# ScalarE rounds x times the norm's weights, and the squares are added by two additions

## What is computed

```python
def rmsnorm(x, g):
    xf = x.astype(jnp.float32)
    y = xf * lax.rsqrt(jnp.mean(xf * xf, axis=-1, keepdims=True) + EPS)
    return (y * g.astype(jnp.float32)).astype(x.dtype)

for i in range(DEPTH):                                    # first block
    x = x + 0.5 * swiglu_ffn(rmsnorm(x, ffn1_norm[i]), ffn1_wi[i], ffn1_wo[i])
    z = rmsnorm(x, mix_norm[i]) @ w_in[i]
    ...
    x = x + mixed @ w_out[i]
    x = x + 0.5 * swiglu_ffn(rmsnorm(x, ffn2_norm[i]), ffn2_wi[i], ffn2_wo[i])
    gate = jax.nn.sigmoid(rmsnorm(x, ple_norm[i]) @ w_ple_gate[i])
    x = x + gate * (p[i] @ w_ple[i])
for l in range(DEPTH):                                    # second block
    h = rmsnorm_2(x, norm_mix_g[l])
    ...
    x = x + mix @ w_out[l]
    x = x + squared_relu_mlp(rmsnorm_2(x, norm_mlp_g[l]), mlp_w1[l], mlp_w2[l])
return rmsnorm_2(x, final_norm_g)
```

## Time and profile before

| | us |
|---|---|
| median of 3 runs | 3871.23 |
| lowest and highest run | 3866.43, 3871.86 |
| span of the profiled execution | 3867.6 |
| its time beside the span | not given; the span is 3.6 under the median |
| PE busy | 3661.1 (95%) |
| POOL busy | 1404.7 (36%) |
| DVE busy | 1841.0 (48%) |
| ACT busy | 1006.2 (26%) |

### The profile page before, as it was taken

One profiled execution on the slowest core, in us unless ns is written; L12 is line 12 of the kernel. 1 busy time (PEld: TensorE's weight loads), 2 busy tenths in 40 slices (PEclk: granted clock), 3 DMA queues, 4 the chain that ended last, 5 costly groups with the idle time before them and its releaser, 6 DMA issues.

```text
span 3867.6 us, 44550 instructions
## 1 busy us (share of the span) xinstructions
PE 3661.1 (95%) x15582; PEld 2828.9 (73%) x15582; DVE 1841.0 (48%) x2258; ACT 1006.2 (26%) x1320; POOL 1404.7 (36%) x581
## 2 busy tenths in 40 slices
PE   3999999999999999999999999898899999889997
PEld 2888865778887788875678888664688876467886
DVE  3542224754424542323665422757463554748163
ACT  1222223322222222222422222333221123322111
POOL 1444432334443444331234443321244432114442
PEclk6999999999999999999999999888999998899998
DMA  3332321223322332231223323211133231113231
GB/s 92 106 98 93 96 68 49 71 82 98 98 97 86 96 96 94 84 90 44 66 78 101 98 98 96 71 32 30 54 104 97 94 87 37 36 44 91 94 98 60
DMA packets 473852, 309.79 MB, mean 80 GB/s; under 512 B 16809, under 2 KB 432531, under 8 KB 473715
## 3 DMA queue, kind: packets, MB, share of 16 engines
q1 hardware_dynamic: 470224, 305.16, 26.4%
q10 hardware_dynamic: 3491, 2.80, 0.5%
HBM read 304.25 MB, written 3.67 MB: 80 GB/s over the span
## 4 chain that ended last, share of the span: by engine, by line
issue 65%; POOL 24%; PE 9%; POOLq 1%; DVE 0%; ACT 0%; DVEq 0%
POOL wl L421 24%; PE bank L444 2%; PE bank L443 2%; PE bank L439 2%; PE bank L462 1%; PE bank L458 1%; PE bank L464 1%; POOLq L420 0%; POOLq L418 0%; PE bank L465 0%; DVE y_sb L2014 0%; PE mb L503 0%; DVE var L1444 0%; DVE var L1424 0%; POOLq L421 0%
## 5 line engine op out<-in xcount | busy, mean ns | idle before, releaser
L421 POOL TENSOR_TENSOR wl<-raw,wh 128x1024 fp32r<-128x1024 f32 x576 | 1404.3, 2440 | 2413.1 <-ACT wh L1093 2412.8
L1093 ACT ACTIVATE wh<-raw 128x1024 fp32r<-128x1024 f32 x576 | 607.1, 1056 | 1626.0 <-PE bank L458 793.6
L458 PE MATMUL bank<-xh,wh 128*128 128x512 f32 x2528 | 995.9, 394 | 3.5 <-DVE xl L1418 3.5
L462 PE MATMUL bank<-xl,wh 128*128 128x512 f32 x2528 | 990.2, 392 | 0.0
L464 PE MATMUL bank<-xh,wl 128*128 128x512 f32 x2212 | 866.5, 392 | 0.0
L458 PEld LDWEIGHTS bank<-xh,wh 128*128 128x128 f32 x2528 | 478.4, 189 | 119.3 <-issue 18.5
L462 PEld LDWEIGHTS bank<-xl,wh 128*128 128x128 f32 x2528 | 478.7, 189 | 99.2
L444 PE MATMUL bank<-hh,wl 128*128 128x512 f32 (+1 forms) x1216 | 485.1, 399 | 0.0
L464 PEld LDWEIGHTS bank<-xh,wl 128*128 128x128 f32 x2212 | 418.8, 189 | 88.8
L443 PE MATMUL bank<-hl,wh 128*128 128x512 f32 (+1 forms) x1216 | 479.2, 394 | 0.0
L439 PE MATMUL bank<-hh,wh 128*128 128x512 f32 (+1 forms) x1216 | 476.8, 392 | 0.0
(11 more groups left out here) (358 smaller groups left out, 3439.5 us busy)
## 6 DMA issues: line engine op xcount, KB each, us to landing
raw<-in_ffn_wi_dram SPq DMA_DIRECT2D x176, 512.0 KB, 3.8
raw<-in_mlp_w_dram SPq DMA_DIRECT2D x128, 512.0 KB, 3.8
raw<-in_w_in_dram SPq DMA_DIRECT2D x102, 512.0 KB, 3.7
raw<-in_ffn_wo_dram SPq DMA_DIRECT2D x88, 512.0 KB, 3.6
raw<-in_w_out_dram SPq DMA_DIRECT2D x32, 512.0 KB, 3.9
raw<-in_w_ple_gate_dram SPq DMA_DIRECT2D x16, 512.0 KB, 3.6
raw<-in_w_a_dram SPq DMA_DIRECT2D x8, 512.0 KB, 3.5
raw<-in_w_b_dram SPq DMA_DIRECT2D x8, 512.0 KB, 3.4
```

Source lines behind the costliest of these rows:

```text
L421: gp.tensor_tensor(wl[j][:], raw[j % RAW_SLOTS][:], wh[j][:].bitcast(F32), ALU.subtract)\
L458: first = pe.matmul(out[0:width, :], h[:, c:c + width], rh[:, k, :], start=k == 0, stop=False)
L462: pe.matmul(out[0:width, :], h[:, c:c + width], rl[:, k, :], start=False, stop=False)
L1093: act.activation(wh[n % SPLIT_SLOTS][:], raw[n % RAW_SLOTS][:], ACT.Copy).then_inc(s.hi_ready, 1)
```

## The change

On ACT, `square_half` is given the norm's weights. Before the Square it makes the `xh` of the half's first two x tiles and after it those of the last two, each by a Copy with a scale for each partition, and signals `xh_ready`. On DVE the `xh` product and its drain are gone, and each `xl` product waits for `xh_ready`. The strided reduction is replaced by an addition of two tiles to two tiles, a drain and an addition of one tile to one. In `first_half` DVE makes two `xl`, then the sum, then the other two, where it made all four ahead of the sum; in `norm` the order (two, sum, two) stays. The calls of `square_half`, `norm` and `ffn` on ACT pass the weights. Nothing else moves, so on ACT four copies stand between `x_final` and what followed the Square: in `norm`, the rounding of slab n+3.

```diff
+            def x_times_gain(j, g):
+                act.activation(xh[:, j, :], x_sb[:, j, :], ACT.Copy, scale=g[:, j:j + 1]).then_inc(s.xh_ready, 1)
 
-            def square_half(B, L, k, half):
+            def square_half(B, L, k, half, g):
                 act.wait_ge(s.x_final, half_no(B, L, k, half))
+                if g is not None:
+                    for j in range(4 * half, 4 * half + 2):
+                        x_times_gain(j, g)
                 if half:
                     act.wait_ge(s.ss_ready, half_no(B, L, k, 0))
                 act.activation(tmp_all[:], x_sb[:, 4 * half:4 * half + 4, :], ACT.Square).then_inc(s.sq_ready, 1)
+                if g is not None:
+                    for j in range(4 * half + 2, 4 * half + 4):
+                        x_times_gain(j, g)
...
-            def x_times_gain(j, g):
-                dve.tensor_scalar(xh[:, j, :], x_sb[:, j, :], g[:, j:j + 1], None, ALU.mult)
-                dve.drain()
+            def x_times_gain(B, L, k, j, g):
+                dve.wait_ge(s.xh_ready, at(L, B.norms * KT, B.base_norm * KT + k * KT + j + 1))
                 dve.scalar_tensor_tensor(out=xl[:, j, :], in0=x_sb[:, j, :], scalar=g[:, j:j + 1],
                                          in1=xh[:, j, :].bitcast(F32), op0=ALU.mult, op1=ALU.subtract)\
                    .then_inc(s.xl_ready, 1)
...
                 dve.wait_ge(s.sq_ready, half_no(B, L, k, half))
-                last = dve.tensor_reduce((acc, var)[half][:], tmp_all[:].rearrange("p j t -> p t j"), AX.X, ALU.add)
+                dve.tensor_tensor(tmp_all[:, 0:2, :], tmp_all[:, 0:2, :], tmp_all[:, 2:4, :], ALU.add)
+                dve.drain()
+                last = dve.tensor_tensor((acc, var)[half][:], tmp[0], tmp[1], ALU.add)
                 if half:
...
                 dve.drain().then_inc(s.x_final, 1)
                 if g is not None:
-                    for j in range(4):
-                        x_times_gain(j, g)
+                    for j in range(2):
+                        x_times_gain(B, L, k, j, g)
                 sum_half(B, L, k, 0)
+                if g is not None:
+                    for j in range(2, 4):
+                        x_times_gain(B, L, k, j, g)
```

More of the change, by code:

```diff
@@ L254, in program @@
             setup_t setup_copied rel_psum toep_row toep_out toep_in consts_ready
-            x_final sq_ready ss_ready ss_psum inv_var rstd_ready xl_ready
+            x_final sq_ready ss_ready ss_psum xh_ready inv_var rstd_ready xl_ready
             silu_done hidden_ready gate_landed gate_split gates_psum gate_pre log1p ml_rows_done emt_done
@@ L1106, in square_half, with norm @@
                 act.activation(tmp_all[:], x_sb[:, 4 * half:4 * half + 4, :], ACT.Square).then_inc(s.sq_ready, 1)
-            def norm(B, L, k, n):
-                square_half(B, L, k, 1)
+                if g is not None:
+                    for j in range(4 * half + 2, 4 * half + 4):
+                        x_times_gain(j, g)
+            def norm(B, L, k, n, g):
+                square_half(B, L, k, 1, g)
                 if n is not None:
@@ L1116, in norm, with ffn @@
                     ahead(B, L, n + 1, 3)
-            def ffn(L, k, n, t, silu0):
-                norm(Block1, L, k, n)
+            def ffn(L, k, n, t, silu0, g, g_next):
+                norm(Block1, L, k, n, g)
                 def pair(f, i=None):
@@ L1134, in ffn @@
                     ahead(Block1, L, n0, 4, i, 4)
-                square_half(Block1, L, k + 1, 0)
+                square_half(Block1, L, k + 1, 0, g_next)
                 with act.Fori(3, 5) as i:
@@ L1221, in gated @@
                 ahead(Block1, L, S_OUT, 5)
-                square_half(Block1, L, 2, 0)
+                square_half(Block1, L, 2, 0, par1[:, R_FFN2:R_FFN2 + KT])
                 ahead(Block1, L, S_OUT + 5, 3)
             def ple(L):
-                norm(Block1, L, 3, S_PLE)
+                norm(Block1, L, 3, S_PLE, par1[:, R_PLE:R_PLE + KT])
                 for j in range(KT):
@@ L1232, in ple @@
                         round_hi(Block1, L, S_PLE + j + AHEAD)
-                square_half(Block1, L, Block1.norms, 0)
+                square_half(Block1, L, Block1.norms, 0, g_first)
             for dst, name in ((rel, "rel_bias"), (onehot, "onehot"), (pad, "pad")):
@@ L1273, in _ @@
                .then_inc(s.toep_in, 16)
-            square_half(Block1, None, 0, 0)
+            square_half(Block1, None, 0, 0, g_first)
             with act.Fori(0, 2) as L:
@@ L1277, in _ @@
                     round_hi(Block1, L, n)
-                ffn(L, 0, S_FFN1, T_FFN1, 0)
-                norm(Block1, L, 1, S_IN)
+                ffn(L, 0, S_FFN1, T_FFN1, 0, g_first, par1[:, R_MIX:R_MIX + KT])
+                norm(Block1, L, 1, S_IN, par1[:, R_MIX:R_MIX + KT])
                 ahead(Block1, L, S_IN + 4, 8)
@@ L1283, in _ @@
                 gated(L)
-                ffn(L, 2, S_FFN2, T_FFN2, FT)
+                ffn(L, 2, S_FFN2, T_FFN2, FT, par1[:, R_FFN2:R_FFN2 + KT], par1[:, R_PLE:R_PLE + KT])
                 ple(L)
@@ L1395, in _ @@
                     round_hi(B, L, n)
-                norm(B, L, 0, S2_IN)
+                norm(B, L, 0, S2_IN, g_first)
                 gmlp(L)
@@ L1400, in _ @@
                 ahead(B, L, S2_OUT, 8)
-                square_half(B, L, 1, 0)
-                norm(B, L, 1, S2_MLP)
+                square_half(B, L, 1, 0, par2[:, Q_MLP:Q_MLP + KT])
+                norm(B, L, 1, S2_MLP, par2[:, Q_MLP:Q_MLP + KT])
                 with act.Fori(1, 2 * FT2 // 4 - 2) as i:
@@ L1405, in _ @@
                 ahead(B, L, B2_SLABS - 8, 2)
-                square_half(B, L, B.norms, 0)
+                square_half(B, L, B.norms, 0, g_first)
                 ahead(B, L, B2_SLABS - 6, 6)
-            norm(Last, None, 0, None)
+            norm(Last, None, 0, None, None)
         @block.vector
```

## The result

The median after is 3887.91 us (four runs, 3885.15 to 3890.14), beside 3869.70 for the kernel before in the same comparison: ratio 1.0049, 95% interval 1.0035 to 1.0063. It is slower, as forecast, and 2.9 us above the 3885 predicted. The forecast stood on a median of 3871.23, so the change itself came to +18.2 us where +14.1 was predicted. The span went from 3867.6 to 3886.5.

What follows compares the result with a forecast made beforehand. PE, busy 95%, loses time where it stands still, chiefly the fourth tile waiting for a slab rounded behind ACT's work. Terms 4.2 + 4.1 + 2.6 + 3.0 + 4.2 - 2.4 - 1.6 = +14.1 us on 3871.23 gave 3885, range 3880 to 3889.

Steps and rivals of the forecast that it cites:

- Startup: Ahead of the first loop: ACT rounds slabs later, so PE's fourth tile starts at 86.65 instead of 82.59, +4.1 us.
- Into Block2: Entry in layer 0: POOL's `wl` pair leaves the reduction's cover and stops DVE's x additions twice, +3.0 us.
- Block2 layer 1, k=0: That norm's fourth tile +2.5 us; PE's gap of 0.58 becomes 3.0, likely a cold restart, +1.7; together +4.2.
- Last norm: Program's last norm: no copies matter, PE waits for the sum, whose reduction becomes two additions, -1.6 us.
- k=1: Block2's norm k=1, in both layers: x final sooner, and PE's restart before the fourth tile warm, -1.2 us each.
- every fourth tile with a PE wait on POOL `wl`: Sign of being right: each fourth tile of `first_units` waits for its weight slab, 0.7 us at six Block1 norms.
- Six Block1 norms: Block1 norms k=1, 2, 3, two layers: copies delay the slab 2.5 us less 1.75 slack, +0.7 each, +4.2.
- 0 where the table below puts no POOL under the additions: Port-contention cost of DVE's additions per half, bounded 0 to 2.4 us, taken as 0 where no POOL runs beside them.
- PLE into layer 1: Entry into layer 1: x final 1.6 us sooner, then copies, fourth tile +0.9; PE's cold restart +1.7; together +2.6.
- Faster: Rival: DVE is what the norms wait for, so its cheaper sum wins; 3858 us, chance 0.12.
- The port lock: Rival: every sum in the open meets a `wl` and DVE gains nothing; about +21 us, 3892, chance 0.08.
- A wash: Rival: copies cost their low end (2.1), two gaps restart warm, collisions into Block2 luckier; +5 us, 3877, chance 0.25.

Runs made afterwards that it cites:

- additions only: The kernel before with only the two additions in place of the strided reduction, no copies on ACT: 3871.71 us, ratio 1.0014.
- copies only: The kernel after with the strided reduction back in both halves; ACT still makes the copies: 3893.42 us, ratio 1.0066.
- copies on the best version: The kernel before with additions in half 1 only, slab n+3 rounded ahead of the Square, and ACT's four copies per half: 3883.11 us, ratio 1.0035.

## Why the prediction was right

**Right, by its steps.** The slab's rounding behind ACT's Square is what the fourth tile waits for (the two kernels that move it take 14.6 and 15.9 us off the table's sum). Startup +4.3 for +4.1, first matmul at 73.97 for 74.0. The fourth tile at startup came at 86.70 for 86.65. Into Block2 +3.3 for +3.0, PE's start there 0.95 later for 1.15; Block2 layer 1, k=0, +4.1 for +4.2, with the cold restart: the matmuls after the wait of 3.14 take 0.63 each. Last norm -1.6 for -1.6. The copies cost 2.45 for 2.5.

**k=1: right in layer 0, by luck in layer 1.** -1.1 and -1.0 were measured for -1.2 (of which the terms given, +0.2 and -1.7, make -1.5). In layer 0 the fourth tile came 0.5 later, behind a wait of 1.82 on `wl`, and PE then ran warm (at its full clock), which won 1.6. In layer 1 PE came out of the second wait on `xl` cold (8 matmuls at 1.2 GHz), and the fourth tile waited for nothing. So of the sign "every fourth tile with a PE wait on POOL `wl`" this one is missing.

**Two terms were mis-sized, and by luck offset each other.** *Six Block1 norms*: 0.7 each predicted, 1.21 measured. The step that failed is "0 where the table below puts no POOL under the additions": it asked only whether `wl` would hold up DVE. At these norms it is DVE's third addition that holds up `wl`, by 0.37. The run with copies alone, where the reduction is back, shows 0.82.

*PLE into layer 1*: +2.6 predicted, +0.3 measured. Its parts failed too. The traces stand 8.08 us apart just before. Against that PE started 0.6 later (1261.34 - 1252.68 - 8.08), not 1.0 sooner. DVE was 2.2 sooner behind half 0, about as predicted, but the two additions ahead of the read that frees PE took 2.52 and 2.06, where they took 1.14 and 0.69: 2.75 more, where the prediction left room for 1.0. The last addition was held too (2.69). Yet x was final 2.5 sooner (predicted 1.6), since something else fell away. After its last addition, at the return of the loop over layers, DVE stood still with no releaser. Timeline of DVE, before:

```profile
1260.09 0.18 DVE L1730 COPY par<-p 128x38 f32 x1 [3.17 <-issue]
```

and after:

```profile
1255.34 2.52 DVE L1736 TENSOR_TENSOR x_sb<-x_sb,gate_sg 128x512 f32<-128x512 f32 x1
...
1258.56 2.06 DVE L1736 TENSOR_TENSOR x_sb<-x_sb,gate_sg 128x512 f32<-128x512 f32 x1
...
1262.69 2.69 DVE L1736 TENSOR_TENSOR x_sb<-x_sb,gate_sg 128x512 f32<-128x512 f32 x1
...
1265.77 0.18 DVE L1744 COPY par<-p 128x38 f32 x1 [0.39 <-issue]
```

The last addition ends 0.4 later, the return takes 2.8 less (0.39 for 3.17), so DVE is 2.4 sooner; then the copies (2.45) and a `wl` of 2.74 instead of 2.35 take it back: +0.3. What DVE does in that time is not shown, but the traces say when it shows. In the four kernels whose last addition took 0.69 (before, additions only, copies only, and copies on the best version) the idle time is 2.37 to 3.55; in the other eight traces `wl` held the last addition for 2.09 to 2.69, and the idle time is 0.39 to 1.25. So the return seems to run beside an addition that is held. With PE's wait at 2.00 instead of the 4.3 predicted, the cold restart (1.7) did not come.

Six norms cost 3.1 more, PLE 2.3 less, the rest agrees within 0.4 each; so the sum came out as 15.6 for 14.1. The prediction had no term for the stages between the norms, where the trace has another 3.5, the largest part with PE's clock. With them the change (+18.2 in the medians, +19.1 in the traces) lies above the +10 to +17 that the ends of the copies' price gave. The time lies within the forecast's 3880 to 3889 also because the kernel before came out 1.5 lower.

**The rivals.** *Faster* falls: with DVE's work taken away and the slab free, the copies still cost 17.7 us in the table (-6.0 to +11.7). *The port lock* got 0.08 and deserved more. Alone, the additions bring -0.7 instead of the -7 I expected of them: the lock eats them at both entries, as that rival said, but not at k=1 or at the last norm. *A wash* needed a ratio of 1.0015; the interval begins at 1.0035.

## What to carry to other kernels

Before work is moved to an idle engine, look at what is queued behind the place where it goes: ACT was idle 74% of the time, and yet its next instruction was the one that TensorE waited for. Before a slow instruction is replaced by faster ones, look at what lies beside it and which ports it leaves alone; a strided reduction of 3.7 us was the cover under which POOL worked undisturbed. Where instructions of two engines collide, ask in both directions who holds up whom, and where the stall goes once it is moved.

## What the runs showed of the hardware

- A shared port works in both directions, and the price depends on who is first. POOL first: DVE's addition of 1.22 took 3.36. DVE first: `wl` took 2.78 instead of 2.41. A reduction beside POOL cost neither more than 0.1: in the kernel before it took 3.62 to 3.82 without POOL and 3.70 to 3.91 beside it, and a `wl` that started under it 2.34 to 2.41.
- Not only two-input instructions are held up. A cast of DVE, one input, in the kernel before, beside a pair of `wl` (POOL's line) and alone:

```profile
3500.25 5.45 POOL L421 TENSOR_TENSOR wl<-raw,wh 128x1024 fp32r<-128x1024 f32 x2 [11.44 <-ACT wh L1093]
...
3501.07 2.37 DVE L1416 CAST hh<-tmp_all 128x512 f32 x1 [0.17 <-issue]
...
3507.82 0.43 DVE L1416 CAST hh<-tmp_all 128x512 f32 x1 [0.19 <-issue]
```

- The length of a wait alone does not tell whether TensorE comes back at half its clock. In the kernel after, two waits at the same place of two layers (timeline, and windows behind them with the columns as above):

```profile
2794.01 0.50 PE L439 MATMUL bank<-xh,wh 128*128 128x512 f32 x1 [2.67 <-DVE xl L1446]
...
3502.04 0.79 PE L439 MATMUL bank<-xh,wh 128*128 128x512 f32 x1 [2.48 <-DVE xl L1446]
```

```profile
3502.00:3505.00 3.00, 2.96 (x7) 2.38 (x8) 2.06 (x3) 2.27 (x3) 0.00 (x0) 0.50 0.00 0
2794.00:2797.00 3.00, 2.99 (x13) 2.42 (x14) 2.03 (x3) 2.30 (x3) 0.00 (x0) 1.00 0.00 0
```

The wait of 2.67 ends at a granted clock of 1.00 (2.4 GHz), that of 2.48 at 0.50 (1.2 GHz). In both layers a wait of 2.37 on `xl` and 6 matmuls came just before.
